# Scoring the key cache in a decoder layer: VectorE block transposes and 32x32 score tiles in place of TensorE transposes and one wide score matmul

## The chip, the cores and the metric

One Trainium2 chip, one of its cores. The metric is the time of one execution on the device in microseconds, from the first to the last instruction and what lies around them.

## The reference, cut to what matters

One layer of a hybrid decoder runs on 256 prompt tokens and on 8 samples of 8 tokens. Everything is float32. The layer is an adaptive norm, one input projection, a gated linear attention (GLA), a block-sparse attention (MoBA), a projection of each, a gated merge, an output projection, and a mixture of 32 experts. The change lies in the attention of the 8 samples over their cached keys and values, 1024 tokens each in 8 pages of 128:

```python
gate = jnp.einsum('bqhd,bjhd->bhqj', qq.astype(jnp.float32), k_mean)   # k_mean: mean of each block of 256 keys
_, top = lax.top_k(gate, n_sel)                                        # 3 of the 4 past blocks, and the own block
logits = jnp.einsum('bqhd,bhqsnd->bhqsn', qq, kg).astype(jnp.float32) * scale
logits = jnp.where(mask, logits, -jnp.inf).reshape(B, H, qc, -1)
p = jax.nn.softmax(logits, axis=-1).reshape(mask.shape).astype(v.dtype)
return jnp.einsum('bhqsn,bhqsnd->bqhd', p, vg)
```

A sample has 8 queries for each of 8 heads of 64 dimensions. The heads go in pairs, so that a pair fills 128 partitions. A block's gate is the sum of its scores, so that all scores are computed and one of the four blocks is masked afterwards.

## The kernel before, in words

Five engines run programs of their own and wait for each other by semaphores; the order of the work on each engine is written out by hand. Big weights and cache pages pass through a ring of six slots of 2 MB in SBUF (`ring`). Slots 0 to 3 serve the numbered items of the early stages (`N_BA`, `N_CACHE`, `N_PROJ`), item n in slot n % 4. SyncE issues nearly all loads in the order of the items and waits before each until the item that had the slot has been used (`used`). GpSimd issues the pages of the cached values (`value_pages`).

The stages in order of time, of which the change touches the second and third:

- up to 275 us: conditioning, norm, input projection and GLA;
- 275 to 328 us, the prompt's attention. It has 8 heads in 4 pairs. TensorE alternates between scores, transposes and value products of the heads and `gate_steps(n)`, eight matmuls of 320 columns that make job n of the merge gates (L814 to L824). For each head VectorE adds the mask, takes two maxima and negates them (L1864 to L1867, `ms_max`), ScalarE takes exponentials (L1414, `ms_exp`), TensorE transposes the probabilities (`prompt_probs`), ScalarE copies them (L1403) and TensorE multiplies them with the values. ScalarE's sigmoid of each gate job is L1365.
- 328 to 449 us, the cache stage, described below;
- 449 to 501 us, projections 8 to 23 (`project`, L990);
- 501 to 525 us, the router; then 32 experts to 1440 us, each with six slots of 2 MB of weights (`gate_up` L1155, `down` L1174, `combine` L1185), and a short end.

The first expert's slots are loaded as the last four items of the early stages are done (SyncE, L511); the stream of expert loads goes on from there, each load behind the use of what its slot held.

**The cache stage.** In the turn of sample b (`cache_turn`) TensorE does:

1. `cache_scores(b)` (L932, L934): for each half of the 1024 tokens and each of the four pairs a matmul with 128x32 weights (the pair's queries `qs`, zero where the other head is) and 512 columns of `kTs`; four pairs stand side by side in the columns of the array. Then the 64 tokens of the samples themselves.
2. `cache_keys(b + 1)` (the transposes are at L584): 32 transposes of 128x128 turn the next sample's keys from token rows to dimension rows, through PSUM banks 0 to 2. ScalarE copies each group of four to `kTs` (L1434, eight copies of 512 columns a sample).
3. `cache_values(b - 1)` (L952, L955): 36 matmuls of 128x32 weights (the turned probabilities `pts`, `pto`) and 128 columns, again four side by side.
4. `turn_steps` (L973): half or all of one projection of the GLA branch, with weights in `aux`.
5. `cache_probs(b)`: nine transposes of the probabilities `pex` (L584), and `cache_out(b - 1)`: one of the scaled output.

Meanwhile VectorE runs `cache_max(b)` (L1887 to L1906): two reductions over 1024 scores in PSUM, then small operations that choose the blocks and give the exponent's bias (`cs_max`). ScalarE takes five exponentials (L1441, `cs_exp`) and copies the first half of the turned probabilities (L1444). VectorE copies the other half (L1913), copies the queries (`queries`, L1879), scales the output (L1917), copies it out (L1924) and merges finished projections (`projected`, L1933).

SyncE's `key_pages(b)` (L486 to L490) reads eight page numbers from the page table and issues eight loads of 256 KB; for b of 2 and more it waits until sample b - 2's keys are turned. Two sets of pages fit in the ring at a time (slots 0 and 2), and two of values (slots 1 and 3). Every weight item is waited for by `land`, and a set of pages only as a whole: its semaphore counts all eight.

Most TensorE instructions show twice in the profile: a float32 matmul is run as two records, a transpose as one.

Of the kernel before, what the change touches and what calls it, by code (L numbers as in the profile page):

```python
# [23 lines left out]
ALU = mybir.AluOpType  # L24
AX = mybir.AxisListType.X

# [118 lines left out]
def decoder_layer(nc, x_prompt, x_sample, cache_k, cache_v, state_gla, page_table, c_prompt, c_sample,  # L145
# [3 lines left out]
    with ExitStack() as ctx:  # L149
# [24 lines left out]
        def const(name):  # L174
# [172 lines left out]
        q_sb, kt2_ps, kt2_sb, cs_ps, cs_max, cs_exp, cp_ps, cp_a, cp_d, co_ps, co_sb, cot_ps, cot_sb = (  # L347
            sem(n) for n in ("q_sb", "kt2_ps", "kt2_sb", "cs_ps", "cs_max", "cs_exp", "cp_ps", "cp_a", "cp_d",
# [15 lines left out]
        x3_sb, rms3_sb, rinv_sb, out_sb = ([sem(f"{w}{t}") for t in range(3)] for w in ("x3_sb", "rms3_sb", "rinv_sb", "out_sb"))  # L364
# [9 lines left out]
        N_PRE = 46  # L374
# [6 lines left out]
        for n, w, c0 in ((N_PROJ, w_proj_gla, 512), (N_PROJ + 2, w_out, 0), (N_PROJ + 3, w_out, 512)):  # L381
            w2d[n] = (w[0], c0)
# [42 lines left out]
        def _(sp):  # L425
# [154 lines left out]
        def _(pe):  # L580
# [230 lines left out]
            def gate_steps(n, bank, k0, k1):  # L811

                it, m = N_BA + (n - 29) // 4, (n - 29) % 4
                if k0 == 0:  # L814
                    wait_item(pe, it)
                    pe.wait_ge(fm_sb, n if bank == 3 else n - 1)
                    if n == 42:
                        pe.wait_ge(ms_max, MH)
# [24 lines left out]
            def gate_bank(n):  # L843

                return n % 2 if n < 42 else 3
# [61 lines left out]
            def probs_copied(n):  # L907

                pe.wait_ge(cp_a, n)
                pe.wait_ge(cp_d, n)  # L910

            TURN_STEPS = ((0, 0, 8), (1, 0, 8), (2, 0, 4), (2, 4, 8), (3, 0, 4), (3, 4, 8))

            def cache_keys(b, half, par, j0=0, j1=2 * PAIRS):

                nk = N_CACHE + 2 * par
                pe.wait_ge(land[nk % PRE], half * (16 * NPAGES) + landed[nk])
                for jj in range(j0, j1):
                    p, f = divmod(jj, 2)
                    if jj >= 3:  # L920
# [1350 lines left out]
```

## Time and profile before

| | us |
|---|---|
| median of 3 runs | 1468.13 (1467.8 to 1472.22) |
| the profiled execution | 1469.78 |
| its span, first to last instruction | 1468.1 |
| TensorE matmuls busy in the span | 1434.4 (98%) |
| VectorE busy | 571.9 (39%) |
| ScalarE busy | 259.0 (18%) |
| GpSimd busy | 43.4 (3%) |
| mean granted TensorE clock | 0.996 |

The DMA engines moved 515.28 MB, 351 GB/s on average. The busy shares are averages over stages with quite different limits; the ends of matmuls in the profile are modelled, so that a busy TensorE is not one at its peak. A matmul's busy time in a timeline line runs to the modelled end of its last instruction and overlaps the next line; the time that a piece costs is better read from the start of one line to the start of the next.

### The profile page before, as it was taken

How to read it: one execution, taken by the hardware profiler on the slowest of the kernel's cores; microseconds unless marked ns; L12 is line 12 of the kernel's file. 1: busy time of each engine (PE TensorE's matmuls, PEld its weight loads, DVE VectorE, ACT ScalarE, POOL GpSimd, SP SyncE). 2: the span in 40 equal slices, each digit the busy share in tenths (PEclk: the TensorE clock that was granted, in tenths of full speed). 3: DMA queues.
4: the chain of work that ended last, by engine and by line, in shares of the span. 5: the costliest groups of instructions: out<-in, count | busy, mean ns of one | idle time of the engine just before them, and what ended most of it. 6: DMA issues, size and time to landing. Idle time of an engine off the chain costs nothing.

```text
span 1468.1 us, 20188 instructions
## 1 busy us (share of the span) xinstructions
PE 1434.4 (98%) x7694; PEld 637.7 (43%) x7694; DVE 571.9 (39%) x1220; ACT 259.0 (18%) x541; POOL 43.4 (3%) x85
## 2 busy tenths in 40 slices
PE   7999999999999999999999999999999999999996
PEld 3644575677777733333333333333333333333332
DVE  4016625424543563334324433432343233323334
ACT  2103034546530231000001000100000010001001
POOL 1100000012320000000000000000000000000000
PEclk9999999999999999999999999999999999999998
DMA  9646447667967498999999999999999999999994
GB/s 363 226 168 229 173 155 252 224 235 247 336 227 282 162 379 333 421 429 428 429 428 429 429 429 429 428 429 429 429 429 429 429 429 428 429 429 429 429 429 201
DMA packets 75283, 515.28 MB, mean 351 GB/s; under 512 B 6259, under 2 KB 15401, under 8 KB 47586
## 3 DMA queue, kind: packets, MB, share of 16 engines
q1 hardware_dynamic: 69682, 497.44, 83.1%
q0 software_dynamic: 5552, 17.16, 3.3%
q8 instruction: 33, 0.54, 0.2%
q14 instruction: 16, 0.13, 0.0%
HBM read 507.24 MB, written 7.34 MB: 351 GB/s over the span
## 4 chain that ended last, share of the span: by engine, by line
PE 41%; DMA 21%; DVE 1%; issue 0%; SPq 0%; DVEq 0%
PE ps L1155 21%; DMA ring<-in_w_gate_up 21%; PE ps L1174 10%; PE ps L1121 3%; PE ps L1185 3%; PE ps L584 2%; PE ps L1137 1%; PE ps L1188 1%; DVE mem L2209 0%; DVE mem L2197 0%; SPq L511 0%; DVE mem L2102 0%; DVE mem L2174 0%; DVE mem L2105 0%; DVE mem L2117 0%
## 5 line engine op out<-in xcount | busy, mean ns | idle before, releaser
L1155 PE MATMUL ps<-ring,mem 128*64 128x512 f32 x2032 | 445.7, 594 | 5.0 <-DMA ring<-in_w_gate_up 4.9
L1155 PEld LDWEIGHTS ps<-ring,mem 128*64 128x64 f32 x2032 | 142.1, 137 | 306.3 <-issue 289.5
L1174 PE MATMUL ps<-ring,mem 128*64 128x512 f32 x1024 | 227.4, 597 | 0.0
L2098 DVE TENSOR_SCALAR mem<-ps 128x512 f32<-128x512 f32 x32 | 22.1, 692 | 413.2 <-PE ps L1155 413.2
L1174 PEld LDWEIGHTS ps<-ring,mem 128*64 128x64 f32 x1024 | 70.8, 137 | 152.6 <-issue 152.6
L2116 DVE TENSOR_TENSOR mem<-ps,mem 128x1024 f32<-128x1024 f32 (+1 forms) x97 | 101.2, 1043 | 40.7 <-PE ps L1185 28.7
L1506 ACT ACTIVATE mem<-mem 128x512 f32<-128x512 f32 x32 | 20.2, 630 | 490.2 <-DVE mem L2098 490.2
L2117 DVE TENSOR_TENSOR mem<-mem 128x1024 f32<-128x1024 f32 (+1 forms) x97 | 101.2, 1043 | 3.3
L1121 PE MATMUL ps<-mem 128*64 128x512 f32 (+1 forms) x384 | 92.7, 600 | 1.3 <-issue 1.3
L584 PEld LDWEIGHTS ps<-mem 128*128 128x128 f32 (+2 forms) x487 | 63.6, 179 | 69.4 <-issue 54.5
L584 PE MATMUL ps<-mem 128*128 128x128 f32 (+2 forms) x487 | 85.7, 303 | 6.0 <-DMA mem<-in_x_sample 2.3
L1185 PE MATMUL ps<-mem 64*128 64x512 f32 x264 | 74.8, 644 | 1.8 <-DVE mem L2139 1.0
L820 PE MATMUL ps<-mem,ring 128*128 128x320 f32 x256 | 75.4, 439 | 0.6 <-issue 0.6
L691 PE MATMUL ps<-ring,mem 128*128 128x512 f32 x160 | 70.1, 595 | 0.0
L990 PE MATMUL ps<-mem,ring 128*128 128x320 f32 x256 | 69.3, 433 | 0.0
L2109 DVE COPY mem<-ps 128x512 f32<-128x512 f32 x31 | 21.4, 692 | 114.3 <-PE ps L1174 114.3
L1502 ACT COPY mem<-ps 128x512 f32<-128x512 f32 x32 | 18.7, 585 | 254.3 <-PE ps L584 254.3
L990 PEld LDWEIGHTS ps<-mem,ring 128*128 128x128 f32 x256 | 48.5, 190 | 20.0
L820 PEld LDWEIGHTS ps<-mem,ring 128*128 128x128 f32 x256 | 46.2, 190 | 20.3 <-issue 4.7
L651 PE MATMUL ps<-mem,ring 128*128 128x320 f32 x192 | 52.2, 433 | 0.0
L1121 PEld LDWEIGHTS ps<-mem 128*64 128x64 f32 (+1 forms) x384 | 24.7, 135 | 62.8 <-issue 62.8
L691 PEld LDWEIGHTS ps<-ring,mem 128*128 128x128 f32 x160 | 30.0, 190 | 38.9 <-issue 38.7
(352 smaller groups left out, 1140.5 us busy)
## 6 DMA issues: line engine op xcount, KB each, us to landing
ring<-in_w_gate_up SPq DMA_DIRECT2D x127, 2048.0 KB, 20.2
ring<-in_w_down SPq DMA_DIRECT2D x64, 2048.0 KB, 18.8
ring<-in_w_ada SPq DMA_DIRECT2D x12, 2048.0 KB, 11.1
ring<-in_w_in SPq DMA_DIRECT2D x12, 2048.0 KB, 11.4
ring<-in_cache_k SPq DMA_DIRECT2D x64, 256.0 KB, 4.7
ring<-in_cache_v POOLq DMA_DIRECT2D x64, 256.0 KB, 5.4
ring<-in_state_gla SPq DMA_DIRECT2D x2, 2048.0 KB, 9.2
out<-ring SPq DMA_DIRECT2D x2, 2048.0 KB, 10.9
```

The costliest lines, as they stand in the source:

```text
L584: return nc.tensor.transpose(out, in_, ident[0:n, 0:n])
L651: last = mm(ps[0:M, n % 3, 0:T], w[:, k, :], hT[:, k, :], start=k == 0, stop=k == KD - 1)
L691: last = mm(ps[0:n, 3 + t, :], hT[:, k, t0:t0 + n], item(N_TM[c])[:, k, :], start=k == 0, stop=k == KD - 1)
L820: last = mm(ps[:, bank, 0:T], item(it)[:, k, m * P:(m + 1) * P], hT[:, k, :], start=k == 0, stop=k == KD - 1)
L990: last = mm(bank, w[:, k, c0:c0 + P], src[:, k, :], start=k == 0, stop=k == kc - 1)
L1121: last = mm(ps[64 * f:64 * f + 64, 0, :], hot[par][0:rows, t, :], h2_tok[0:rows, t, 512 * f:512 * f + 512], start=t == 0, stop=t == 2)
L1155: last = mm(out, xeT[:, 2 * (s % 2) + k, s // 2, :], w[:, k, 512 * q:512 * q + 512], start=False, stop=s == 3 and k == 1)
L1174: last = mm(ps[64 * f:64 * f + 64, 0, :], actT[:, k, s, :], w[:, k, 512 * f:512 * f + 512], start=s == 0 and k == 0, stop=s == 1 and k == 3)
L1185: last = mm(ps[:, bank + f, :], spread[par][rows, t0:t0 + n], y[rows, :], start=True, stop=True)
L2098: v.tensor_scalar(glu, ps[:, 2, :], LIMIT, None, ALU.min).then_inc(glu_sb, 1)
L2116: return (v.tensor_tensor(y.rearrange("p (f d) -> p f d", f=2), ps[:, bank:bank + 2, 0:w], g.rearrange("p (f d) -> p f d", f=2), ALU.mult) ...
L2117: lambda: v.tensor_tensor(x, x, y, ALU.add))
```

## The change: what it does

- **Keys.** They are no longer turned by TensorE. VectorE transposes them in place in the ring slot, in blocks of 32x32, in four strided pieces a sample (`keys_turned`; piece g holds dimensions 32g to 32g + 31 of every pair's 128, 32 blocks of 32 elements, 1024 elements in each of 128 partitions). The pieces for sample 0 stand behind heads 4 to 7 of the prompt's attention, those for sample b + 1 behind `cache_max(b)`. ScalarE's copies to `kTs` and `kTs` itself go.
- **Queries.** `queries_spread` multiplies the samples' queries with 32-column pieces of the identity (16 matmuls of 256 columns), so that each of the four row groups has each piece; ScalarE copies them once to `q_rep` and for each sample to `qz` and `qs` (`cache_queries`).
- **Scores.** 64 matmuls of 32x32 weights and 256 columns, 4 row groups (32 tokens of each page) by 4 pairs by 4 pieces that accumulate. Row group i writes to bank 4 + i. Four own-token matmuls as before.
- **Order on TensorE.** Scores of b + 1 stand behind the values of b - 1 and ahead of the transposes of b's probabilities; each turn has a whole projection (`turn_project`). At the start: spread queries, job 43, scores 0, job 44, probabilities 0, scores 1. Jobs 42 to 44 use banks 0 and 1.
- **Elsewhere.** ScalarE does all copies of turned probabilities, the scaling and the output. The second half of the GLA projection's weights goes to `aux2` by a load of its own on SyncE's queue, ahead of the pages of sample 2, and the ring has one item fewer (`N_PRE` 45). Key pages b + 2 wait for the scores of b. The base of the router uses bank 4. One array of three semaphores in the last stage becomes one.

The diff, cut to its core:

```diff
-        kTs = part(mem, g0, PAIRS, PAGE * NPAGES)
+        aux2 = part(mem, g0, KD, 512)
         pex = part(mem, g0 + 4096, PAGE * NPAGES + NS_TOK)
         pts = part(mem, g0 + 5184, NPAGES, P)
+        q_rep = part(late, 5120, 4, PAIRS, NS_TOK)
         pto = part(mem, g0 + 6208, P)
         qs = part(mem, g0 + 6336, PAIRS, 32)
         osm = part(mem, g0 + 6464, P)
+        qz = part(mem, g0 + 6592, 4, PAIRS, 32)
...
-            used[N_CACHE + 2 * b], used[N_CACHE + 2 * b + 1] = (kt2_ps, 8 * b + 8), (co_ps, b + 1)
-        for j, jobs in enumerate((8, 16, 20, 24)):
+            used[N_CACHE + 2 * b], used[N_CACHE + 2 * b + 1] = (cs_ps, b + 1), (co_ps, b + 1)
...
+            sp.wait_ge(mot_ps, 1)
+            sp.dma_start(aux2, w_proj_gla[0][:, 512:1024].rearrange("(k p) n -> p k n", p=P)).then_inc(side_in, 16)
             with sp.Fori(1, NB // 2) as i:
                 for par in range(2):
                     b = i * 2 + par
-                    sp.wait_ge(kt2_ps, b * 8 - 8)
+                    sp.wait_ge(cs_ps, b - 1)
...
+            def queries_spread():
+
+                pe.wait_ge(mo_sb, MH)
+                for g in range(4):
+                    for i in range(4):
+                        last = mm(ps[32 * i:32 * i + 32, 6 + g // 2, BLOCK * (g % 2):BLOCK * (g % 2 + 1)], ident[:, 32 * g:32 * g + 32],
+                                  mqT[:, :, NP_TOK:T], start=True, stop=True)
+                last.then_inc(qr_ps, 1)
 
             def cache_scores(b):
 
-                pe.wait_ge(kt2_sb, b * 8 + 8)
-                pe.wait_ge(q_sb, b + 1)
-                for f in range(2):
+                keys = item(N_CACHE + 2 * (b % 2))
+                pe.wait_ge(qz_sb, b + 1)
+                for g in range(4):
+                    pe.wait_ge(kb_sb, 4 * b + g + 1)
                     for p in range(PAIRS):
-                        mm(ps[32 * p:32 * p + 32, 4 + f, :], qs[:, p, :], kTs[:, p, 512 * f:512 * f + 512], start=True, stop=True)
+                        c0 = p * P + 32 * g
+                        for i in range(4):
+                            rows = slice(32 * i, 32 * i + 32)
+                            mm(ps[32 * p:32 * p + 32, 4 + i, 0:BLOCK], qz[rows, g, p, :], keys[rows, :, c0:c0 + 32],
+                               start=g == 0, stop=g == 3)
                 for p in range(PAIRS):
-                    last = mm(ps[32 * p:32 * p + 32, 6, 0:NS_TOK], qs[:, p, :], mkT[:, p, NP_TOK:T], start=True, stop=True)
+                    last = mm(ps[32 * p:32 * p + 32, 4, BLOCK:BLOCK + NS_TOK], qs[:, p, :], mkT[:, p, NP_TOK:T], start=True, stop=True)
                 last.then_inc(cs_ps, 1)
...
+            def turn_project(n):
+
+                if n == 0:
                     pe.wait_ge(side_in, 32)
-                    if n:
-                        pe.wait_ge(pj_sb, n)
-                    else:
-                        pe.wait_ge(fm_sb, 45)
-                for k in range(k0, k1):
-                    last = mm(ps[:, 3, 0:T], aux[:, k, n * P:n * P + P], oTg[:, k, :], start=k == 0, stop=k == KD - 1)
-                if k1 == KD:
-                    last.then_inc(pj_ps, 1)
+                    pe.wait_ge(fm_sb, 45)
+                    pe.wait_ge(ms_max, MH)
+                if n == 4:
+                    pe.wait_ge(side_in, 48)
+                if n:
+                    pe.wait_ge(pj_sb, n)
+                w = (aux, aux2)[n // 4]
+                for k in range(KD):
+                    last = mm(ps[:, 3, 0:T], w[:, k, (n % 4) * P:(n % 4 + 1) * P], oTg[:, k, :], start=k == 0, stop=k == KD - 1)
+                last.then_inc(pj_ps, 1)
...
+            queries_spread()
+            gate_steps(43, gate_bank(43), 0, KD)
             pe.wait_ge(mot_sb, 2)
             cache_scores(0)
-            cache_keys(1, 0, 1)
             gate_steps(44, gate_bank(44), 0, KD)
-            cache_probs(0, 16)
-
-            def cache_turn(b, half, par):
-
-                cache_scores(b)
-                probs_copied(b)
-                cache_keys(b + 1, half + par, 1 - par)
+            pe.wait_ge(fm_sb, 45)
+            cache_probs(0)
+
+            for b in range(1, NB):
+                if b == 1:
+                    cache_scores(1)
+                turn_project(b - 1)
+                pe.wait_ge(cp_sb, b)
                 pe.wait_ge(cot_sb, b)
-                cache_values(b - 1, half + par - 1, 1 - par)
-                turn_steps(*TURN_STEPS[b - 1])
-                cache_probs(b, b * 8 + 16)
+                cache_values(b - 1)
+                pe.wait_ge(cs_exp, b + 1)
+                if b + 1 < NB:
+                    cache_scores(b + 1)
                 cache_out(b - 1)
-
-            for b in range(1, NB - 1):
-                cache_turn(b, b // 2, b % 2)
-            cache_scores(NB - 1)
-            probs_copied(NB - 1)
-            for n in range(4, 7):
-                project(n)
-            pe.wait_ge(cot_sb, NB - 1)
-            cache_values(NB - 2, NB // 2 - 1, 0)
+                cache_probs(b)
...
+            def cache_queries(b):
+
+                if b:
+                    act.wait_ge(cs_ps, b)
+                for hh in range(2):
+                    a.copy(qz[:, 2 * hh:2 * hh + 2, :, 8 * hh:8 * hh + 8], q_rep[:, 2 * hh:2 * hh + 2, :, LS * b:LS * b + LS])
+                for hh in range(2):
+                    rows = slice(64 * hh, 64 * hh + 64)
+                    last = a.copy(qs[rows, :, 8 * hh:8 * hh + 8], mqT[rows, :, NP_TOK + LS * b:NP_TOK + LS * b + LS])
+                last.then_inc(qz_sb, 1)
...
+            act.wait_ge(qr_ps, 1)
+            for f in range(2):
+                a.copy(q_rep[:, 2 * f:2 * f + 2], ps[:, 6 + f, :].rearrange("p (g a b) -> p g a b", g=2, b=NS_TOK)).then_inc(act_step, 1)
+            act.wait_ge(act_step, 17)
+            cache_queries(0)
             gate(43)
-            cache_keys(1)
+            cache_queries(1)
+            gate(44)
             cache_exp(0)
-            cache_keys(2)
-            gate(44)
-            cache_exp(1)
-            with act.Fori(2, NB - 1) as b:
-                cache_keys(b + 1)
+            probs_copied(0)
+            for b in range(1, NB):
+                if b + 1 < NB:
+                    cache_queries(b + 1)
                 cache_exp(b)
-            cache_exp(NB - 1)
+                cache_scale(b - 1)
+                cache_out(b - 1)
+                probs_copied(b)
+            cache_scale(NB - 1)
+            cache_out(NB - 1)
...
+            def keys_turned(b, pieces):
+
+                nk = N_CACHE + 2 * (b % 2)
+                dve.wait_ge(land[nk % PRE], b // 2 * (16 * NPAGES) + landed[nk])
+                for j in pieces:
+                    x = ring[:, nk % PRE, :].rearrange("p (a g d) -> p a g d", g=4, d=32)[:, :, j, :]
+                    v.transpose(x, x).then_inc(kb_sb, 1)
...
+                if h >= 4:
+                    keys_turned(0, (h - 4,))
...
+            for b in range(NB):
                 cache_max(b)
-                queries(b + 1)
-                cache_scale(b - 1)
-                if b in (1, 2, 4, 6):
-                    projected((0, 1, 2, 2, 3, 3)[b - 1])
-                cache_probs(b)
-                cache_out(b - 1)
-            cache_max(NB - 1)
-            for n in range(4, 7):
-                projected(n)
-            cache_scale(NB - 2)
-            cache_probs(NB - 1)
-            cache_out(NB - 2)
+                if b + 1 < NB:
+                    keys_turned(b + 1, range(4))
+                else:
+                    dve.wait_ge(qz_sb, NB)
+                    shifts()
+                if b:
+                    projected(b - 1)
+                cache_den(b)
```

## Rows read from the trace of the kernel before

**Rows 1.** The chain that ended last: start us, us, what (loads of the last stage).

```profile
1089.30 25.20 DMA ring<-in_w_gate_up
...
1412.12 25.44 DMA ring<-in_w_gate_up
```

**Rows 2.** SyncE's waits from 280 to 620 us: who waited for whom, total, times, longest.

```profile
SPq L511 <- PE ps L990: 55.3, 4, 16.9
```

**Rows 3.** Busy time of the engines by stretch, granted clock, DMA share, GB/s.

```profile
core 0: us, PE busy (x) PEld busy (x) DVE busy (x) ACT busy (x) POOL busy (x), PEclk, DMA share, GB/s
360.00:370.00 10.00, 10.00 (x143) 7.53 (x141) 6.22 (x22) 6.01 (x15) 3.00 (x6) 1.00 1.05 389
...
505.00:510.00 5.00, 5.00 (x32) 4.11 (x34) 3.38 (x17) 1.62 (x4) 0.00 (x0) 0.66 0.97 373
```

**Rows 4.** Timeline of TensorE, one turn and three projections: start us, us, instruction.

```profile
398.34 1.92 PE L932 MATMUL ps<-mem 128*32 128x512 f32 x16
...
400.31 3.95 PE L584 MATMUL ps<-mem,ring 128*128 128x128 f32 x32
404.18 1.95 PE L952 MATMUL ps<-ring,mem 128*32 128x128 f32 x64
...
406.29 2.42 PE L973 MATMUL ps<-mem 128*128 128x320 f32 x8
408.54 1.25 PE L584 MATMUL ps<-mem 128*128 128x128 f32 x10
409.73 1.92 PE L932 MATMUL ps<-mem 128*32 128x512 f32 x16
...
423.08 13.19 PE L990 MATMUL ps<-mem,ring 128*128 128x320 f32 x48
```

**Rows 5.** Timeline of TensorE, matmuls on tiles that differ in their rows.

```profile
263.82 0.71 PE L808 MATMUL ps<-mem 32*128 32x256 f32 x8
...
557.43 1.09 PE L1137 MATMUL ps<-mem 32*64 32x512 f32 x8
```

**Rows 6.** Timeline of VectorE and ScalarE: the maxima and exponentials of one sample.

```profile
343.10 1.28 ACT L1441 ACT_TABLE_LOAD   x1
...
364.13 1.23 DVE L1887 TENSOR_REDUCE mem<-ps 128x4 f32<-128x1024 f32 x1 [1.05 <-PE ps L934]
...
365.27 1.22 DVE L1888 TENSOR_REDUCE mem<-ps 128x4 f32<-128x1024 f32 x1
...
368.48 0.23 DVE L1906 TENSOR_SCALAR mem<-mem 128x4 f32<-128x4 f32 x1
...
368.74 0.47 ACT L1441 ACTIVATE mem<-ps,mem 128x256 f32<-128x256 f32 x1
...
370.79 0.21 ACT L1441 ACTIVATION_READ_ACCUMULATOR mem<-ring,mem 128x1 f32 x1
```

**Rows 7.** Timeline of VectorE: 1024 elements from SBUF to SBUF.

```profile
1447.80 1.23 DVE L2117 TENSOR_TENSOR mem<-mem 128x1024 f32<-128x1024 f32 x1
```

**Rows 8.** The line that issues key pages, 300.5 to 301.5 us: last page of sample 0.

```profile
L490 SPq DMA_DIRECT2D ring<-in_cache_k x1: 337/337/337, 300.6 to 300.6; - x1
...
DMA to landing us min/median/max: 11.9/11.9/11.9
```

**Rows 9.** Timeline of the prompt's head 5: VectorE, ScalarE's exponentials, TensorE's transposes.

```profile
300.50 0.56 DVE L1864 TENSOR_TENSOR mem<-ps,mem 128x384 f32<-128x384 f32 x1
...
301.74 0.17 DVE L1867 TENSOR_SCALAR mem<-mem 128x2 f32<-128x2 f32 x1
...
303.08 0.39 ACT L1414 ACTIVATE mem<-mem 128x128 f32<-128x128 f32 x1
...
303.87 0.18 ACT L1414 ACTIVATION_READ_ACCUMULATOR mem<-mem 128x1 f32 x1
...
304.88 0.49 PE L584 MATMUL ps<-mem 128*128 128x128 f32 x3
```

**Rows 10.** Timeline of TensorE at the start of the program.

```profile
16.56 3.64 PE L613 MATMUL ps<-ring,mem 128*32 128x512 f32 x16
...
21.50 3.99 PE L613 MATMUL ps<-ring,mem 128*32 128x512 f32 x32
```

More of the change, by code:

```diff
@@ L25 @@
 AX = mybir.AxisListType.X
+AXY = mybir.AxisListType.XY
 P = 128
@@ L904, in _ @@
             gate_steps(42, gate_bank(42), 4, KD)
[L907 to L920, printed above, removed]
-                        pe.wait_ge(kt2_sb, b * 8 + jj - 2)
-                    for q in range(4):
-                        last = tr(ps[:, jj % 3, q * P:(q + 1) * P], item(nk)[:, 4 * f + q, p * P:(p + 1) * P])
-                    last.then_inc(kt2_ps, 1)
+            def queries_spread():
[5 more added lines that the diff above has]
+                last.then_inc(qr_ps, 1)
@@ L1027, in _ @@
             for m in range(KD):
-                mm(ps[:, 3, 0:NE], modT[:, 3, m, 0:1].to_broadcast([P, P]), w_rt[:, m, :], start=m == 0, stop=m == KD - 1)
+                mm(ps[:, 4, 0:NE], modT[:, 3, m, 0:1].to_broadcast([P, P]), w_rt[:, m, :], start=m == 0, stop=m == KD - 1)
             for m in range(KD):
-                last = mm(ps[0:NS_TOK, 3, NE:2 * NE], sh_x[:, m, :], w_rt[:, m, :], start=m == 0, stop=m == KD - 1)
+                last = mm(ps[0:NS_TOK, 4, NE:2 * NE], sh_x[:, m, :], w_rt[:, m, :], start=m == 0, stop=m == KD - 1)
@@ L1436, in cache_exp @@
             def cache_exp(b):
                 act.wait_ge(cs_max, b + 1)
-                for j in range(NBLK + 1):
-                    c0, c1 = (BLOCK * j, BLOCK * (j + 1)) if j < NBLK else (PAGE * NPAGES, PAGE * NPAGES + NS_TOK)
-                    src = ps[:, 4 + j // 2, (j % 2) * BLOCK:(j % 2 + 1) * BLOCK] if j < NBLK else tmp[:, 0:NS_TOK]
-                    last = a.activation(pex[:, c0:c1], src, ACT.Exp, scale=HD ** -0.5, bias=colB[:, j:j + 1], accum_out=colC[:, j:j + 1])
-                last.then_inc(cs_exp, 1)
@@ L1443, in cache_exp @@
-                act.wait_ge(cp_ps, b + 1)
-                a.copy(pts[:, 0:4, :], ps[:, 0, :].rearrange("p (a b) -> p a b", b=P))
-                a.copy(pto[0:NS_TOK, :], ps[0:NS_TOK, 2, 0:P]).then_inc(cp_a, 1)
-            gate(42)
-            cache_keys(0)
+                scores = ps[:, 4:8, 0:BLOCK].rearrange("p i (j t) -> p i j t", t=32)
+                probs = pex[:, 0:PAGE * NPAGES].rearrange("p (j i t) -> p i j t", i=4, t=32)
+                for j in range(NBLK):
+                    a.activation(probs[:, :, 2 * j:2 * j + 2, :], scores[:, :, 2 * j:2 * j + 2, :], ACT.Exp, scale=HD ** -0.5,
+                                 bias=colB[:, j:j + 1], accum_out=colC[:, j:j + 1])
@@ new lines, in cache_out @@
+            def cache_out(b):
+                act.wait_ge(cot_ps, b + 1)
+                for hh in range(2):
+                    rows = slice(64 * hh, 64 * hh + 64)
+                    src = ps[rows, 2, 0:P].rearrange("p (a r) -> p a r", r=32)[:, :, 8 * hh:8 * hh + 8]
+                    last = a.copy(oTm[rows, :, NP_TOK + LS * b:NP_TOK + LS * b + LS], src)
+                last.then_inc(cot_sb, 1)
+            gate(42)
+            act.wait_ge(qr_ps, 1)
+            for f in range(2):
+                a.copy(q_rep[:, 2 * f:2 * f + 2], ps[:, 6 + f, :].rearrange("p (g a b) -> p g a b", g=2, b=NS_TOK)).then_inc(act_step, 1)
@@ L2201, in _ @@
             dve.wait_ge(last_sb, 1)
-            second().then_inc(x3_sb[2], 1)
+            second().then_inc(x3_sb, 1)
             for t in range(3):
```

136 lines of the change are left out of this document (55 added, 81 removed).

## Prediction, made before the changed kernel was run

> **What bounds the kernel now.** I read the chain of waits first. From 1089 us on, twelve hand-overs in a row end with a load of w_gate_up (25 us each) and 3.7 us of matmuls, one expert about every 29.3 us [rows 1]: the last third is paced by its loads. Does a gain at 330 to 450 us then reach the end? A load starts only when its ring slot is free. SyncE's own waits say who frees them: the four loads of expert 0 waited 55.3 us in all for the projections' matmuls [rows 2]. So the stream of loads starts where TensorE lets it, and a shift of the projections shifts it and the end one for one. The slot released last is still one whole slot after job 24.
>
> In the cache stage TensorE is busy 10.00 of 10 us, at a granted clock of 1.00, while the DMA engines are full too, at 389 GB/s [rows 3]. One turn (a sample) in TensorE's timeline [rows 4], start to start: scores 1.97, key transposes 3.87, values 2.11, half a projection 2.25, probabilities and output 1.19, together 11.39 us. A whole projection is 13.19/3 = 4.40. Nothing is idle, so what is taken from TensorE here is worth its full length until another chain takes over.
>
> **What goes.** Eight key turns, 8 x 3.87 = 31.0, and eight old scores, 8 x 1.97 = 15.8: 46.8 us. ScalarE's copies of the turned keys go too, beside TensorE, and are worth nothing. Jobs 42 to 44 no longer wait in bank 3: the 0.6 us or so ahead of job 42 go.
>
> **What comes on TensorE.**
> - The spread queries: 32 instructions of 256 columns, four side by side. The old scores take 1.92 us for 16 of 512 columns [rows 4], so 0.06 each: 1.9 us, once.
> - The new scores: 64 matmuls of 32x32 weights and 256 columns, so 128 instructions. The row of the old scores is 4 rounds of 512 columns on four tiles, 0.43 us a round, 0.215 for 256 columns. If all 16 tiles work at once, 8 rounds are 1.7 us; with the four own-token matmuls and the change of tile shape I take **2.15 us**. No row has 16 tiles. The nearest with row groups are four 32-row tiles (8 instructions of 256 columns in 0.71 us) and 32x64 tiles (8 of 512 columns in 1.09 us) [rows 5]; one at a time they would be 1.7 and 3.4 us, so tiles that differ in rows do overlap, with different banks. Four at once only would be 128 x 0.054 + 0.4 = 7.2 us; that is the upper end, 1.9 the lower. I stay near the lower because both rows show no loss beyond a start of some 0.2 us.
>
> The Trainium skill ("TensorE: Matmul & The Clock Gate", Measured speedup vs the span model) gives 10.6x, not 16x, for 16 tiles. By that the scores would be nearer 2.9 us and my sum some 5 us higher; no run here shows it yet.
>
> **The new loop.** Scores of b end; VectorE's maxima take 4.58 us (364.13 to 368.71) and ScalarE's exponentials 2.26 (368.74 to 371.00) [rows 6], so exp is there after 7.0. VectorE then turns keys b+1 in four pieces of 1024 elements. No row transposes on VectorE. The nearest: 1024 elements from SBUF 1.23 us [rows 7]; the next starts 1.14 after a 1.23 one [rows 6]. Lower end 1.14; upper end twice that, if 4-byte transposing runs at half rate; I take 1.14, the plain rate. The last piece is there at 0.07 + 4.5 + 4 x 1.14 + 0.1 = 9.2, then its quarter of the scores, the own-token ones and the drain, 0.9: **10.1 us a turn**. TensorE's work is 1.19 + 4.40 + 2.11 + 2.15 = 9.85. So it idles 0.25 us in six turns, 1.5 us. VectorE's turn, 4.6 + 4.6 + a projection 0.5 + denominators 0.4, equals the loop: it becomes the tight engine. ScalarE (query copies about 0.9, exp 2.26, scale and output 0.8, probability copies 1.4, by the rows' sizes) has room.
>
> **Queues.** Keys and values are 4.2 MB a turn; at 389 GB/s [rows 3] that is 10.8 us, more than 10.1. Key pages b+2 are asked for when scores b end, have a turn plus 4.6 us to land, and the first ones have a head start; I work that out as at most 1 to 2 us late in the last turns, kept for the range. The extra weight load stands on SyncE's queue after the second set of pages, and lands long before job 4.
>
> **First and last turn.** The first probabilities now stand ahead of scores 1, and behind job 44. Job 44 takes 4.4; ScalarE's sigmoid for it, a table load of 1.28 [rows 6] and exp 2.26 end about 8.6 after scores 0. TensorE, which had the keys of sample 1 to turn, is idle **4.2 us**. At the end, scale and copy on ScalarE each show once: 1.0 net.
>
> Stage: -46.8 - 0.6 + 1.9 + 8 x 2.15 + 1.5 + 4.2 + 1.0 = **-21.6 us**.
>
> **The added wait.** VectorE turns piece 0 of keys 0 behind head 4 of the prompt, and waits first for all eight pages. Head 4 is done at 300.5 us. The last page is issued at 300.6 and takes 11.9 us to land [rows 8]: 312.5. Everything of VectorE queues behind: head 5 (1.41 us, 300.50 to 301.91), its exponentials (1.0), then TensorE's transposes of head 5, which stood at 304.88; all of them are in [rows 9]. Now: 312.5 + 1.2 (the piece) + 1.4 + 1.0 + 0.1 = 316.2, so TensorE stands still for **11.3 us**. The other pieces fit in gaps. Before, these pages were not wanted until 328.5, so their landing cost nothing. Nothing in the change moves their issue.
>
> **Clock.** After idle time TensorE runs at 1.2 GHz: at the start dense matmuls took 3.64 us for 16 and, from 21.5 us, 3.99 for 32 [rows 10], so some 5 us at half speed, 2.5 us lost; at 505 to 510 us, behind a short lull, the granted clock was 0.66 [rows 3]. I add 2.5 after the 11.3 us stop and 1.0 for the 4.2 us one, between 0 and 2.5 each.
>
> **Sum:** -21.6 + 11.3 + 3.5 = -6.8 us. The profiled execution took 1469.8 us (span 1468.1), 1.7 above the median of 1468.1; against it 1463.0, against the median 1461.3. I say **1461.5**. Differences under 0.3% (4.4 us) can hardly be measured here.
>
> **Rivals.**
> - *Tiles at the rate of issue* (slower). Issue, not the array, sets the 32x32 matmuls. Values issue 72 instructions in 2.11 us, 0.029 each [rows 4], the fastest long row there is; 128 are 3.75, scores 4.15. TensorE then sets the turn, 11.85: 6 x 1.75 + 2 x 2.0 = 14.5 more, 1476. It decides from scores of about 2.8 us on. For: no row issues faster over so many. Against: that row is itself held by four tiles of 128 columns, 0.027 each. Chance 0.20. (The same Trainium skill page, in the part on the 56 ns gap, puts a floor of some 25 ns between starts of matmuls; by that 3.2 us and about +7.)
> - *Slow transposes*: 2.3 us a piece. Then VectorE's loop is 14.7, 28 more: 1490. Chance 0.08.
> - *Row groups one after another*: scores 7.2, 39 more: 1500. Against it stand [rows 5]. Chance 0.05.
> - *The wait is short*: pages land earlier, or less queues behind: 1448 to 1457. Only the landing row speaks, and it is clear. Chance 0.12.
> - *It does not pass through*: some load or a later wait takes the rest, 1468. [Rows 2] speak against. Chance 0.10.
> - The forecast, 1457 to 1467: 0.45.
>
> **Numbers.** The range 1453 to 1478 holds the forecast, no change, most of the issue rival and the near part of the short wait. Faster: 0.7 of 0.45 and the short wait, about 0.42; same: the rest of the forecast's middle and no pass-through, 0.22; slower 0.36.
>
> **What would show it.** After: TensorE idle 10 to 12 us near 305 us behind VectorE, which waits for in_cache_k; a granted clock of 0.5 just after; a wait of about 4 us ahead of the first probability transposes; turns of 10 us whose 128 score instructions take 1.8 us; VectorE transposes of 1.1 to 1.25 us; projections of the gates' stage some 7 us earlier, and the same distance from there to the end. Wrong if scores take over 2.8 us, a piece over 1.5, or the stop is under 8 us.

## The result, and the profile after

The changed kernel takes 1474.84 us (median; 1473.19 to 1478.23), the kernel before, on the same chip, 1467.8 us (1467.32 to 1472.22): ratio 1.0047, 95% interval [1.0037, 1.0057]. It is 7.0 us slower, where 6.8 us less was forecast. The profiled execution took 1474.84 us, its span 1473.2 us, so 5.1 us more than the span before.

I read the trace after in the order of the prediction's steps. First the added wait, in the timelines of VectorE and then TensorE (start us, us, instruction, idle before it and its releaser); before, they ran through here [rows 9].

```profile
300.45 0.17 DVE L1900 TENSOR_SCALAR mem<-mem 128x2 f32<-128x2 f32 x1
312.42 1.25 DVE L1876 STREAM_TRANSPOSE ring<-ring 128x1024 f32<-128x1024 f32 x1 [11.80 <-DMA ring<-in_cache_k]
...
303.83 1.24 PE L824 MATMUL ps<-mem,ring 128*128 128x320 f32 x4
316.03 0.90 PE L590 MATMUL ps<-mem 128*128 128x128 f32 x3 [10.96 <-ACT mem L1403]
316.72 3.81 PE L824 MATMUL ps<-mem,ring 128*128 128x320 f32 x8
```

VectorE stands before its first key transpose until the pages of sample 0 have landed, and TensorE behind it until 316.03 us (forecast: until 316.2). ScalarE's L1403 is only the last link. The eight gate matmuls behind the stop take 3.81 us where they took 2.32.

Next the cache stage in TensorE's timeline (compare [rows 4]).

```profile
340.75 1.93 PE L916 MATMUL ps<-mem 128*32 128x256 f32 x32
342.61 4.57 PE L824 MATMUL ps<-mem,ring 128*128 128x320 f32 x16
347.12 2.76 PE L930 MATMUL ps<-ring,mem 32*32 32x256 f32 x128
349.81 0.32 PE L933 MATMUL ps<-mem 128*32 128x64 f32 x8
350.06 4.57 PE L824 MATMUL ps<-mem,ring 128*128 128x320 f32 x16
358.82 2.15 PE L590 MATMUL ps<-mem 128*128 128x128 f32 x9 [4.19 <-ACT mem L1437]
360.91 4.08 PE L930 MATMUL ps<-ring,mem 32*32 32x256 f32 x128
...
385.72 0.31 PE L933 MATMUL ps<-mem 128*32 128x64 f32 x7
388.45 0.32 PE L933 MATMUL ps<-mem 128*32 128x64 f32 x1 [2.42 <-issue]
388.70 2.40 PE L590 MATMUL ps<-mem 128*128 128x128 f32 x10
...
434.07 1.27 PE L930 MATMUL ps<-ring,mem 32*32 32x256 f32 x38 [2.24 <-issue]
435.27 0.32 PE L933 MATMUL ps<-mem 128*32 128x64 f32 x8
435.52 2.19 PE L590 MATMUL ps<-mem 128*128 128x128 f32 x10
...
456.82 8.58 PE L991 MATMUL ps<-mem,ring 128*128 128x320 f32 x31 [0.51 <-issue]
```

The score set runs from 347.12 to 350.06, 2.94 us (forecast 2.15). The first gap is 4.19 us (forecast 4.2). New are two standstills of 2.42 and 2.24 us **in the middle of a run of small matmuls**, put down to "issue": no engine, load or semaphore in the trace ended them. From one own-token matmuls' end to the next (365.17 to 435.52) six turns take 10.2, 13.3, 11.9, 10.6, 10.9 and 13.4 us, not 10.1; the first has no transposes in it, 1.15 us less work than the others.

The windows show the granted clock (the last three columns are clock, DMA share and GB/s).

```profile
309.50:319.70 10.20, 3.67 (x9) 2.67 (x10) 3.61 (x6) 3.44 (x8) 0.00 (x0) 0.50 0.11 38
357.30:364.10 6.80, 5.28 (x109) 4.00 (x111) 2.20 (x4) 2.60 (x11) 3.21 (x7) 0.50 0.99 369
386.00:388.00 2.00, 0.03 (x3) 0.00 (x0) 0.00 (x0) 0.00 (x0) 1.07 (x2) 1.00 1.05 393
388.00:391.40 3.40, 2.95 (x12) 2.62 (x13) 2.56 (x4) 0.63 (x3) 1.54 (x3) 0.50 0.97 337
435.80:439.20 3.40, 3.40 (x14) 2.78 (x13) 3.25 (x9) 1.58 (x5) 1.52 (x3) 0.50 0.88 300
505.00:510.00 5.00, 5.00 (x28) 3.10 (x27) 2.58 (x11) 0.76 (x2) 0.22 (x1) 1.00 0.19 39
```

The standstill itself (386 to 388) has a granted clock of 1.00. With each idle time of over 2 us goes a stretch at 0.50, the 1.2 GHz level, of 10.2, 6.8, 3.4 and 3.4 us; the first three begin while TensorE is still idle, so that 3.7, 5.3 and 2.9 us of them fall on work. The last row is no longer the router's stage, as it was before [rows 3], but still projections. The router's stage begins at 508.67 us now, and from 510 to 522 us its granted clock is 1.00 too: the lull's half clock is gone. VectorE's transposes by their line (durations in ns, minimum, median, maximum), and SyncE's waits, which answer to [rows 2]:

```profile
L1876 DVE STREAM_TRANSPOSE ring<-ring x32: 1201/1204/1246, 312.4 to 431.0; 128x1024 f32<-128x1024 f32 x32
```

```profile
SPq L517 <- PE ps L991: 56.0, 3, 22.2
```

**Where the time went.** The spread queries start at 340.75 us; the key transposes that stood in their place before started at 328.46: +12.3 us. The cache stage, from there to projection 8, is 116.1 us where it was 121.0 (328.5 to 449.5): -5, against a forecast of some -20 with its clock term. So +7.3 at projection 8; the half clock of before in the router's stage costs nothing now, and +5.1 arrive at the end. What is missing from the gain is in the stage.

### The profile page after: what moved, and what is told of

The parts are those of the page before. It is cut to its first block, busy times and chain, and to the rows that moved or that the text cites. A ratio compares the mean times of both kernels' runs of the same rounds, so it can differ in the third digit from the quotient of the medians.

```text
span 1473.2 us, 21424 instructions
## 1 busy us (share of the span) xinstructions
PE 1418.0 (96%) x8366; PEld 624.4 (42%) x8366; DVE 594.4 (40%) x1205; ACT 240.1 (16%) x541; POOL 43.5 (3%) x85
## 4 chain that ended last, share of the span: by engine, by line
PE 39%; DMA 22%; DVE 1%; issue 0%; SPq 0%; DVEq 0%
DMA ring<-in_w_gate_up 22%; PE ps L1144 20%; PE ps L1163 9%; PE ps L1110 3%; PE ps L1174 3%; PE ps L590 2%; PE ps L1126 1%; PE ps L1177 1%; DVE mem L2214 0%; DVE mem L2202 0%; SPq L517 0%; DVE mem L2107 0%; DVE mem L2179 0%; DVE mem L2110 0%; DVE mem L2122 0%
## 5 line engine op out<-in xcount | busy, mean ns | idle before, releaser
L2103 DVE TENSOR_SCALAR mem<-ps 128x512 f32<-128x512 f32 x32 | 22.1, 691 | 413.5 <-PE ps L1144 413.5
L824 PE MATMUL ps<-mem,ring 128*128 128x320 f32 x256 | 76.7, 446 | 0.0
L824 PEld LDWEIGHTS ps<-mem,ring 128*128 128x128 f32 x256 | 47.4, 194 | 20.7 <-issue 5.1
L991 PE MATMUL ps<-mem,ring 128*128 128x320 f32 x192 | 51.9, 433 | 0.5 <-issue 0.5
L657 PE MATMUL ps<-mem,ring 128*128 128x320 f32 x192 | 52.2, 433 | 0.0
L2239 POOL DMA_DIRECT2D ring<-in_cache_v x64 | 34.5, 539 | 365.6 <-issue 365.6
```

The costliest lines, as they stand in the source:

```text
L657: last = mm(ps[0:M, n % 3, 0:T], w[:, k, :], hT[:, k, :], start=k == 0, stop=k == KD - 1)
L824: last = mm(ps[:, bank, 0:T], item(it)[:, k, m * P:(m + 1) * P], hT[:, k, :], start=k == 0, stop=k == KD - 1)
L991: last = mm(bank, w[:, k, c0:c0 + P], src[:, k, :], start=k == 0, stop=k == kc - 1)
L2239: pool.dma_start(item(n)[:, j, :], v_pages[bass.ds(page, 1)].rearrange("o s n -> s (o n)")).then_inc(v_land[par], 16)
```

## The experiments

The ratios are to the kernel before, run on the same chip each time.

### All four pieces of sample 0 behind the prompt's last head

```diff
-                if h >= 4:
-                    keys_turned(0, (h - 4,))
...
+            keys_turned(0, range(4))
```

> The changed kernel, with all four pieces of sample 0's keys turned behind the prompt's last head instead of behind heads 4 to 7. Theory A (the added wait): VectorE no longer stands still from 300.6 to 312.4 us, so TensorE's 10.96 us of idle time goes, and with it the half clock behind it (eight matmuls took 3.81 instead of 2.32 us, and the transposes 0.4 more): 11.2 + 1.9 = 13.1 us faster than the changed kernel, 1461.7. The four pieces fit in between VectorE's end of the prompt at about 321 us and the first scores. Rival B (the wait only hides another one, such as ScalarE's or the pages of sample 1): less than 5 us gained, over 1470. Rival C: the cache stage behind it gets longer, since its pages are no longer early relative to it: 1464 to 1468.

1461.89 us, ratio 0.996 [0.9947, 0.9974], 13.0 us below the change as made. TensorE's timeline has no stop at 304 to 316 us and the eight gate matmuls at 304.94 take 2.32 us again. The rest of the stage is much as before this edit: the first gap of 4.19 us, and three standstills put down to "issue" in the score sets, of 2.3, 0.7 and 1.3 us. So the placing of the first pieces costs 13 us, about what was forecast for stop and clock (13.8).

### The kernel before, with that wait alone

```diff
+                    if h == 4:
+                        dve.wait_ge(land[N_CACHE % PRE], landed[N_CACHE])
```

> The kernel before, with nothing added but VectorE's wait for sample 0's key pages behind head 4 of the prompt. Theory A: TensorE stands still 10 us (no transpose of 1.2 us stands between) and runs about 1.9 us slower behind it: 1467.8 + 10 + 1.9 = 1479.7. Rival B: the wait alone costs little, under 1472.

1479.88 us, ratio 1.0076 [1.0061, 1.0091]: 11.5 us more. The same stop stands in TensorE's timeline (9.96 us here, since no transpose stands behind the wait), with the clock at 0.50 for 10.2 us:

```profile
303.30 1.24 PE L820 MATMUL ps<-mem,ring 128*128 128x320 f32 x4
314.51 0.90 PE L584 MATMUL ps<-mem 128*128 128x128 f32 x3 [9.96 <-ACT mem L1414]
```

Taken away it gives 13.0, added alone it costs 11.5: the term and its pass-through to the end are shown from both sides.

The runs from here start from the kernel of the first experiment, called **the late kernel** below.

### Fewer bytes of values

```diff
-                    pool.dma_start(item(n)[:, j, :], v_pages[bass.ds(page, 1)]...
+                    pool.dma_start(item(n)[:, j, 0:64], v_pages[bass.ds(page, 1), :, 0:64]...
```

Left out: seven eighths of the cached values' columns.

> The kernel with late pieces (e1), and value pages of which only 64 of the 512 columns are loaded (an eighth of the bytes; the sampled tokens' attention output is made of what else stands in the slots). It asks why TensorE stood still twice, 2.4 and 2.2 us, amid the scores with nothing it waits for in the profile, each time about 1.3 us behind the landing of a 16 KB read of instructions and with the DMA engines full. Theory D (instructions arrive late because the DMA engines are full of pages): both gaps and the half clock behind them go, 4.6 + 3 us, about 1454 against 1461.7 for e1. Rival E (TensorE eats its instructions faster than they are ever read, full DMA engines or not): the gaps stay, 1460 to 1462.

1458.37 us, ratio 0.9921 [0.9903, 0.9939]. TensorE's waits (in all, times, longest), with the DMA engines at 194 GB/s from 330 to 460 us where the late kernel has 286:

```profile
PE ps L930 <- issue: 2.7, 1, 2.7
PE ps L933 <- issue: 1.3, 1, 1.3
```

The standstills stay with much less traffic, so full DMA engines don't make them. Yet the run is 3.5 us faster. Its profile has no half clock behind the standstills: the projection behind the first takes 4.47 us where it takes 6.16 in the late kernel, 1.7 of the 3.5 us. Why the clock stayed up isn't shown.

### TensorE kept at work in the first gap

```diff
+            pe.wait_ge(ms_max, MH)
+            keep_warm(7)
```

> The kernel with late pieces (e1), and seven matmuls of 320 columns whose result nobody reads in the gap ahead of the first probability transposes (4.19 us idle in the changed kernel). Theory F (the half clock of that gap costs): the transposes fall from 2.15 to 1.3 us and the scores of sample 1 from 4.08 to 2.76, 2.1 us faster than e1, 1459.6. Rival: the clock does not fall there in every run, or the time is made up in the waits behind it: within 0.5 us of e1.

1459.27 us, ratio 0.9936 [0.9921, 0.9951], 2.6 below the late kernel. Seven matmuls without use fill the gap, and what stands behind keeps its clock:

```profile
341.87 3.93 PE L636 MATMUL ps<-mem 128*128 128x320 f32 x14
346.22 1.18 PE L590 MATMUL ps<-mem 128*128 128x128 f32 x9 [0.42 <-ACT mem L1439]
347.33 2.76 PE L930 MATMUL ps<-ring,mem 32*32 32x256 f32 x128
```

The nine transposes take 1.11 us from start to start and not 2.09, the scores 2.76 and not 4.08: 2.3 us. The two kernels' intervals just touch, and the late kernel's profile has a stretch at 0.50 in the router's stage too (515.8 to 519.2 us) where this one has none; so the rows show the price of the gap, and the times alone would not.

### Every projection a turn earlier

```diff
-            pe.wait_ge(fm_sb, 45)
+            turn_project(0)
...
-                turn_project(b - 1)
+                turn_project(b)
...
-            turn_project(NB - 1)
...
-                if b:
-                    projected(b - 1)
+                projected(b)
```

> The kernel with late pieces (e1, 1461.9), with every projection of the cache stage one turn earlier: projection 0 stands in the gap ahead of the first probability transposes (4.2 us idle), projection b in turn b, and none behind the values of sample 7. Theory H (the gap is free room for TensorE): the 4.4 us of projection 7 at the end go, the clock stays up in the gap (2.6 us, as the unused matmuls showed), the output of sample 7 shows 0.6 us more: 6 us faster than e1, 1456. Rival I (VectorE's loop sets the turns, so what leaves one end comes back at the other): 1459 to 1462.

1456.36 us, ratio 0.9918 [0.9906, 0.9931]. The work put into the gap is work that was needed at the end, so both the gap and its half clock go. Nothing is left out of this version, and it **beats both kernels**: 12 us (0.8%) under the kernel before, 18 under the change as made.

### Half the columns in each score matmul

```diff
-                mm(ps[32 * p:32 * p + 32, 4 + i, 0:BLOCK], qz[rows, g, p, :], keys[rows, :, c0:c0 + 32],
+                mm(ps[32 * p:32 * p + 32, 4 + i, 0:BLOCK // 2], qz[rows, g, p, :], keys[rows, 0:4, c0:c0 + 32],
```

Left out: pages 4 to 7 of each sample's scores.

> The kernel with late pieces (e1), with score matmuls of 128 columns instead of 256, as many instructions as before (the scores of pages 4 to 7 are left out, and what stands in PSUM is used in their place). The 128 score instructions take 2.7 us, 0.021 each, where 16 tiles at full rate would take 0.0135. Theory J (the rate of instructions sets it): the row stays at 2.5 to 2.7 us, the time within 1 us of 1461.9. Rival K (the array, with some loss among 16 tiles, sets it): the row falls to about 1.4 us and the kernel is 6 to 8 us faster. The standstills of TensorE that nothing explains stay in either case, since the instructions are as many.

1462.55 us, ratio 0.9951 [0.9933, 0.9969]: no gain. The time is that of the first reading, the score row that of neither. The 128 instructions take 1.90 us, 15 ns each, where 256 columns take 2.76, 21.6 ns each: columns count, but not in proportion. What was saved came back as waits for VectorE's pieces (groups of TensorE's instructions: busy, mean ns, then the idle time before them):

```profile
L930 PE MATMUL ps<-ring,mem 32*32 32x128 f32 x1024 | 18.0, 300 | 7.8 <-DVE ring L1876 6.4 <-issue 1.0 <-ACT mem L1437 0.4
```

That alone doesn't put the blame on VectorE. In the first turn, where it waits for no page, its last piece comes 0.6 us late, so its loop does stand close behind TensorE's, as forecast. But the rest, 5.8 of the 6.4 us, falls in the three turns in which VectorE itself waited for key pages, 7.0 us in all and 3.4 the longest (2.0 us in all in the late kernel). The prediction had kept 1 to 2 us for late pages in its range; once the turns get shorter, the pages hold them up more than VectorE's own work does.

### The order of the tiles

```diff
-                    for p in range(PAIRS):
-                        c0 = p * P + 32 * g
-                        for i in range(4):
-                            rows = slice(32 * i, 32 * i + 32)
+                    for i in range(4):
+                        rows = slice(32 * i, 32 * i + 32)
+                        for p in range(PAIRS):
+                            c0 = p * P + 32 * g
```

> The kernel with late pieces (e1), with the loops of the score tiles exchanged: four pairs (columns of the array) inside, four row groups outside. If the rate is that of instructions or of the array as a whole, the row stays at 2.7 us and the time at 1461.9 within 1 us. If neighbours in the same columns hinder each other (four PSUM banks, one set of partitions), the row falls towards 1.8 us and the kernel is 4 to 6 us faster; if neighbours in the same rows do, it rises to 3.5 us and more.

1464.72 us, ratio 0.9973 [0.9961, 0.9984]; its interval overlaps the late kernel's. The set still takes 2.76 us, and the standstills stay (2.0 and 0.7 us). A miss that closes one door: the order is of no account.

### Half the pieces in the scores

```diff
-                for g in range(4):
+                for g in range(2):
...
+                pe.wait_ge(kb_sb, 4 * b + 4)
```

Left out: the scores of the second head of each pair, whose dimensions are in pieces 2 and 3.

> The kernel with late pieces (e1), with the scores of pieces 0 and 1 alone, 64 instead of 128 score instructions a turn (the second head of each pair is left out of the scores); VectorE turns all four pieces as before. Theory L (the standstills come from the supply of instructions, a turn's score burst being too dense for it): they go, 4.3 us and about 1.7 us of half clock, and with the shorter row (1.35 us) two first scores and six turns 0.7 us each: 1461.9 - 6.0 - 2.7 - 4.2 = 1449. Rival (they have another cause): the gaps stay, 1455.

1456.29 us, ratio 0.9907 [0.9891, 0.9923]. With 64 instructions a set no standstill is left; the longest waits are now the pages and the pieces:

```profile
PE ps L952 <- DMA ring<-in_cache_v: 4.9, 2, 4.5
PE ps L934 <- DVE ring L1877: 4.2, 4, 1.5
PE ps L590 <- ACT mem L1438: 4.2, 1, 4.2
PE ps L930 <- DVE ring L1877: 2.7, 4, 1.8
```

The expected 1449 didn't come: page transfers, which the prediction had kept for its range, hold the turns up next. Most of the waits for pieces are of that kind too: 5.7 of their 6.9 us stand in the two turns in which VectorE waited for key pages, 6.3 us in all.

### More instructions, hardly more columns

```diff
+                            if g == 0:
+                                for k in range(4):
+                                    mm(ps[32 * p:32 * p + 32, 4 + i, 0:16], qz[rows, g, p, :], qz[rows, 0, 0, 0:16],
+                                       start=True, stop=True)
```

> The kernel with all four pieces of sample 0 behind the prompt's last head, and ahead of the scores of every turn's first piece 64 more matmuls of 32x32 weights and 16 columns (128 instructions a turn) whose results the real ones overwrite. Sixteen columns are a sixteenth of 256, so if the array's work sets the length of the scores (2.76 us for 128 instructions of 256 columns), these add at most 0.2 us a turn, 1.5 us in all: 1463.5. If a fixed rate of starts sets it, they cost what the shorter matmuls did, 15 ns each or more: 1.9 us a turn, and as much of it as VectorE's turn does not hide, 8 to 15 us: 1470 to 1477. If the standstills put down to issue come from the supply of instructions, there are more of them or longer ones, in nearly every turn (before this edit 2.3, 0.7 and 1.3 us in eight turns), with more reads of instructions in the queues, and the time is over 1470; if they have another cause they stay at two or three of the same length.

1491.89 us, ratio 1.0163 [1.0142, 1.0184], 30.0 us above the late kernel and far beyond what I had expected. The first score set takes 6.5 us (335.47 to 341.97) where it took 2.7 to the same point. Of that 0.6 us is a standstill, so 128 instructions of 16 columns add 3.2 us, 25 ns each; eight sets give some 25 us, and more standstills most of the rest. Sixteen columns cost no less than 256 did (21.6 ns), so at this length an instruction is paid for and not its columns. These instructions stand four in a row on one tile, though, and the run doesn't tell what they would cost spread over all 16; there, half the columns did save time. TensorE's waits from 330 to 480 us:

```profile
PE ps L934 <- issue: 3.8, 5, 1.4
PE ps L932 <- issue: 3.2, 3, 1.9
PE ps L937 <- issue: 0.9, 1, 0.9
```

Nine standstills with 7.9 us where the late kernel has three with 4.3. The queue that reads instructions has, over the whole span, 39 reads in the late kernel and 47 here (packets, MB, share):

```profile
q8 instruction: 47, 0.77, 0.2%
```

The program has 2048 more recorded instructions (23472 against 21424) and 8 more reads of 16 KB: one read for 256. The run with half the pieces says the same from the other side, 1024 records and 4 reads fewer. A score set is 128 matmul and 128 weight-load records, so it uses up one such read in 2.8 us.

**Where the standstills are.** With that number I counted all of TensorE's records in the trace up to each standstill: matmuls, weight loads and the semaphore waits between them (103 of the first 4801 are neither matmul nor weight load).

| kernel | records ahead of each standstill |
|---|---|
| the change as made | 4801, 6593 |
| late kernel | 4801, 6081, 6593 |
| fewer bytes; kept at work; order of tiles | 4801, 6593 |
| half the columns | 4801, 5569, 6593 |
| projections earlier | 4801 |
| more instructions | 3777, 4289, 5057, 5569, 5825, 6337, 7105, 7873, 8385 |

Any two of these numbers, in any kernels, differ by a multiple of 256, the size of a read. It is the count that matters and not the place in the work: the matmuls that fill the gap are 28 records more, and the standstill after 4801 records came among the scores there, not at the last own-token matmul. A window from the one standstill of the changed kernel to the other shows the distance nearly, by its counts. Seven of the 898 matmuls had started before it; 891, the 892 weight loads and 9 waits, which the row doesn't count, are 1792, or 7 x 256:

```profile
385.90:431.60 45.70, 43.06 (x898) 31.65 (x892) 36.60 (x81) 19.30 (x80) 16.98 (x32) 0.96 1.00 360
```

And the reads: of the changed kernel's, one starts at 386.01 us, 0.2 us after TensorE's last record ahead of the first standstill (385.81), and takes 1.09 us; TensorE goes on 1.35 us later. The same holds for the second (431.46, 431.66, 1.09, 1.32 us). TensorE had used up its instructions, and the next block was asked for only then.

In other kernels the late block was often asked for a little sooner, and the reads then give the rule. I matched each block with its read, in order, in the traces of all twelve kernels, the next experiment's included, from 320 to 460 us. At 24 block ends TensorE stood still for over 0.5 us from record to record, the standstills of the table. There the read had started at most 2.08 us before TensorE came to the end of its records (in six of them at that moment or up to 0.5 us after it), and TensorE went on 1.25 to 1.54 us after the read had landed. At the 161 other block ends the read had started at least 2.13 us before.

### Projection matmuls between the pieces

```diff
-                turn_project(b)
+                turn_project(b, 0, KD if b + 1 == NB else 5)
...
-                    cache_scores(b + 1)
+                    cache_scores(b + 1, lambda g: turn_project(b, 5 + g, 6 + g) if g < 3 else None)
```

This starts from the kernel with the projections a turn earlier. The same instructions stand in another order, so that a score set comes in four lots.

> The kernel with all four pieces of sample 0 behind the prompt's last head and every projection a turn earlier (1456.4), and in the turns of samples 1 to 6 three of the projection's eight matmuls stand one each between the four pieces of the scores, not ahead of the values. The work is the same; the 128 instructions of a score set come in four lots of 32 with 0.57 us of wide matmuls between them. If the standstills put down to issue come from too many instructions in too short a time, the one left (1.7 us, with the half clock behind it some 3 us) goes, and some of the waits for VectorE's pieces with it (1.1 us): 1452. If the number of instructions alone counts, as many stay as before: 1456. If the array loses time at every change of tile shape, by more than 0.1 us each, the 36 changes cost 4 us or more: 1460.

1460.6 us, ratio 0.9946 [0.9929, 0.9963]. By the time alone that is the third reading, the change of tile shape. The trace says otherwise. TensorE's waits first, then a piece of one turn in its timeline:

```profile
PE ps L930 <- ACT mem L1438: 6.8, 6, 2.0
PE ps L590 <- ACT mem L1451: 1.2, 2, 0.6
PE ps L976 <- issue: 0.6, 1, 0.6
```

```profile
383.93 0.73 PE L930 MATMUL ps<-ring,mem 32*32 32x256 f32 x32 [1.03 <-ACT mem L1438]
384.59 0.81 PE L976 MATMUL ps<-mem 128*128 128x320 f32 x2
385.32 0.72 PE L930 MATMUL ps<-ring,mem 32*32 32x256 f32 x32
...
388.74 0.34 PE L934 MATMUL ps<-mem 128*32 128x64 f32 x8
```

No standstill is left in any score set, and five turns take 12.1 to 12.6 us (364.68 to 425.84), one much like the other. They are longer because fewer matmuls stand ahead of the scores, and these may not overwrite their banks before ScalarE's exponentials have read them: about 1.0 us of waiting in each turn. The changes of shape cost some 0.4 (383.93 to 388.74 is 4.81 us; less three matmuls of 0.57, an eighth of 4.57, 3.10 are left, against 2.69). So both expected effects are there, and a third, not expected, decides the time.

## Why the prediction was wrong, point by point

- **Added wait**: right. TensorE resumed at 316.03 (forecast 316.2); shown from both sides by 13.0 and 11.5 us, with the clock behind it.
- **Pass-through**: right in the main: +7.3 us at projection 8 became +5.1 in the span and 7.0 in the medians (the profiled execution of before lay 1.7 above its median). Of the 2.2 us between, 1.5 are in the router's stage, 23.6 us before with the half clock of [rows 3] (501.20 to 524.80) and 22.1 after (508.67 to 530.72); the rest wasn't followed.
- **VectorE's transposes**: 1.20 us (forecast 1.14, and 1.2 for the first). No row had shown one; the plain rate held, and *slow transposes* fell.
- **First gap**: 4.19 us (forecast 4.2). **What goes** and the spread queries (1.86 us): right.
- **The clock term in the stage** was too small: 1.0 us taken for the first gap, about 2.3 measured by filling it, and nothing was foreseen for the other two half-clock stretches, since nothing was foreseen to make TensorE stop there.
- **The scores**: the first step that failed. 2.94 us where 2.15 were taken, within the bounds (1.9 to 7.2). The step reasoned that the rows of four tiles "show no loss beyond a start"; for 16 tiles an instruction costs 21.6 ns, and not 13.4 (1.72 us for 128). The Trainium skill's "TensorE: Matmul & The Clock Gate", in Measured speedup vs the span model, has 10.6x for 16 tiles, hence the 2.9 us cited in the prediction: the trace agrees, with 2.94. Its floor of some 25 ns between starts (Wait — 56ns, not 53.3ns?) doesn't hold here from tile to tile: 15 ns with 128 columns.
- **"Turns of 10 us"**: the second step that failed. Undisturbed turns take 10.6 us (400.59 to 411.19); two were broken by standstills, which no rival named: the forecast counted instructions by the array's time alone, not by how fast the program can be read, and so put these stops, 4.7 us, and the half clock behind them, 3.9 us, at nothing.

The stage was to take 101.0 us (121.0, less 21.0 without the piece ahead of job 42, plus 1.0 of clock) and took 116.1. The 15.1 us, from the trace:

| | us |
|---|---|
| scores: two sets outside the turns by 0.8 each, six turns by 0.5 each (10.6, not 10.1) | 4.6 |
| two standstills | 4.7 |
| half clock behind them | 3.9 |
| first gap: half clock of 2.3, less the 1.0 taken | 1.3 |
| left: small waits in the turns and at the end | 0.6 |

The six turns are 70.35 us. Five of 10.1 and one without transposes, 8.95, would be 59.45; of the 10.9 more, 3.0 are by the scores, 4.7 by the standstills, and 1.0 by small waits: 0.7 in the first turn, mostly for ScalarE's exponentials, and 0.3 for a piece. That leaves 2.2 for the clock. The transposes and the projection behind the second standstill (435.52 to 442.75) take 7.23 us where an undisturbed pair (400.59 to 406.14) takes 5.55: 1.7 more.

Of the rivals, **tiles at the rate of issue** came nearest in time (1476, measured 1474.84) and its condition was met (scores over 2.8 us). But its price, 29 ns an instruction, was too high, and the scores' length gives 4.6 of the 15.1 us only: the time agrees largely for another reason. What it had in common with the truth is that many small instructions are not free. *Row groups one after another*, *the wait is short* and *no pass-through* fell. The value lies inside the stated range; the forecast and its sign do not hold.

The standstills' cause is shown by the counts, the reads and the last runs: TensorE comes to the end of a block of 256 records before the next one, asked for less than some 2.1 us ahead, can be used. A score set uses up a block in 2.8 us, which leaves little over that. **Still open** is what decides when a block is asked for, and so how to foresee which of them comes late; traffic on the DMA engines isn't the main thing, as the run with fewer bytes shows.

## What to carry to other kernels

Splitting matmuls into 32x32 tiles turns array time into instructions: count them, take 15 to 22 ns each when all 16 tiles are at work (128 and 256 columns here), and allow for standstills where a stretch uses up a few hundred records within 3 us or so. Before work is moved to an engine that others queue behind, look when its data lands: one early transpose cost 13 us here, and put four heads later it turned a loss into a gain. Fill an unavoidable gap with work that is needed anyway, since the gap costs the slower clock behind it too.

## What the runs showed of the hardware that was not expected

- 128 dense instructions on 16 tiles took 2.76 us with 256 columns and 1.90 with 128, and 128 more of 16 columns, four in a row on a tile, added 3.2 us without the standstill in them: far from proportional to the columns.
- TensorE's program is read in blocks of 16 KB, 256 records here. At some block ends it stood still for 0.3 to 2.7 us in a dense run of small matmuls; the trace names no releaser ("issue"), but the count of the records gives it away, and so does the read: it started at most 2.08 us before the block was wanted, and TensorE went on 1.25 to 1.54 us after its landing.
- A standstill of 2.2 us was enough for 3.4 us at the 1.2 GHz level behind it, and one of 1.7 us in the kernel with the projections earlier; behind those of 1.3 and 2.7 us in the run with fewer bytes the granted clock stayed at 1.00.
